# Gated linear attention on one NeuronCore: the scalar engine's side work moved one level behind its exponentials, and every gate made among the first head's levels

## The reference, cut to what matters

```
q, k, v, g, glr, mq = split(hn @ a_w_in)                    # 1024 prompt tokens + 8 sample tokens
log_a = log_sigmoid(glr @ a_w_gate2 + a_b_gate) / 16        # per token, 4 heads x 128 channels
# recurrence, evaluated in chunks:
S_t = diag(exp(log_a_t)) S_{t-1} + k_t^T v_t                # 128 x 192 per head
o_t = q_t S_t
o = rms_norm(o) * silu(g)
```

## Time and profile before

| what | us |
|---|---|
| median of three runs | 2727.14 |
| profiled execution, its own time | 2724.67 |
| span of the profiled execution | 2722.9 |
| PE busy in the span | 2523.3 |
| GLA levels, first scores (404.31) to the last step's transposes (623.83) | 219.5 |
| tail, to the first product of the output projection (650.27) | 26.4 |

### The profile page before, as it was taken

The page is one execution under the profiler, slowest core; times in us unless marked ns, Lnnn a source line. Parts: engine busy times, 40 slices in busy tenths (PEclk is TensorE's granted clock), DMA queues, the critical chain, the costliest instruction groups (busy, mean ns, idle before and its releaser), DMA issues.

```text
span 2722.9 us, 40392 instructions
## 1 busy us (share of the span) xinstructions
PE 2523.3 (93%) x16277; PEld 2413.8 (89%) x16277; DVE 1106.9 (41%) x1685; ACT 510.8 (19%) x1096; POOL 924.1 (34%) x460
## 2 busy tenths in 40 slices
PE   3899977768999999999999789999899999999999
PEld 3899975667999999999999778776899999999998
DVE  6421214645453333333333666623743333333333
ACT  2322113343120000000001434122310000000000
POOL 6333333222323333333334333300233333333332
PEclk9999996889999999999999899979899999999999
DMA  4110131113111111111111310320011111111112
GB/s 174 58 39 32 51 128 36 38 37 130 47 40 47 46 46 46 46 46 46 46 46 47 128 51 32 122 109 1 32 37 47 45 47 45 45 46 46 47 46 75
DMA packets 40994, 154.92 MB, mean 57 GB/s; under 512 B 4784, under 2 KB 11440, under 8 KB 38592
## 3 DMA queue, kind: packets, MB, share of 16 engines
q1 hardware_dynamic: 29760, 107.54, 11.6%
q10 hardware_dynamic: 11136, 45.97, 4.4%
HBM read 135.17 MB, written 18.33 MB: 56 GB/s over the span
## 4 chain that ended last, share of the span: by engine, by line
PE 88%; DVE 8%; ACT 2%; issue 1%; ACTq 0%; DMA 0%; POOL 0%; DVEq 0%; SPq 0%; POOLq 0%
PE bank L576 25%; PE bank L578 25%; PE bank L577 25%; PE bank L770 2%; DVE xt L1664 1%; PE bank L1160 1%; PE bank L1135 1%; PE bank L1155 1%; PE bank L1023 1%; PE bank L1132 1%; PE bank L600 1%; PE bank L655 1%; PE bank L635 1%; PE bank L984 0%; PE bank L643 0%
## 5 line engine op out<-in xcount | busy, mean ns | idle before, releaser
L576 PE MATMUL bank<-x_hi,w_hi 128*128 128x344 f32 (+1 forms) x3304 | 1072.4, 325 | 35.7 <-DVE x_lo L1697 12.5
L577 PE MATMUL bank<-x_lo,w_hi 128*128 128x344 f32 (+1 forms) x3304 | 1058.3, 320 | 0.0
L578 PE MATMUL bank<-x_hi,w_lo 128*128 128x344 f32 (+1 forms) x3304 | 1057.9, 320 | 0.0
L479 POOL TENSOR_TENSOR w_hi<-w_raw,zero 128x1024 fp32r<-128x1024 f32 x187 | 360.9, 1930 | 1534.0 <-PE bank L578 1478.5
L576 PEld LDWEIGHTS bank<-x_hi,w_hi 128*128 128x128 f32 x3304 | 626.6, 190 | 50.8 <-issue 48.0
L577 PEld LDWEIGHTS bank<-x_lo,w_hi 128*128 128x128 f32 x3304 | 625.8, 189 | 1.8 <-issue 0.7
L578 PEld LDWEIGHTS bank<-x_hi,w_lo 128*128 128x128 f32 x3304 | 626.0, 189 | 0.0
L481 POOL TENSOR_TENSOR w_lo<-w_raw,w_hi 128x1024 fp32r<-128x1024 f32 x187 | 461.2, 2466 | 14.7
L1985 DVE TENSOR_TENSOR hid<-sil,bank 128x344 f32<-128x344 f32 x132 | 67.7, 513 | 779.8 <-PE bank L578 742.3
L576 PE MATMUL bank<-hid_hi,w_hi 128*128 128x344 f32 x1056 | 340.1, 322 | 0.0
L577 PE MATMUL bank<-hid_lo,w_hi 128*128 128x344 f32 x1056 | 337.7, 320 | 0.0
(11 more groups left out here) (302 smaller groups left out, 1787.6 us busy)
## 6 DMA issues: line engine op xcount, KB each, us to landing
w_raw<-in_w SPq DMA_DIRECT2D x187, 512.0 KB, 3.4
h<-in_x ACTq DMA_DIRECT2D x3, 1376.0 KB, 15.3
h_spill<-h ACTq DMA_DIRECT2D x1, 4128.0 KB, 11.8
h<-h_spill ACTq DMA_DIRECT2D x1, 4128.0 KB, 13.7
out_y<-h ACTq DMA_DIRECT2D x3, 1376.0 KB, 5.7
g_spill<-ring ACTq DMA_DIRECT2D x6, 516.0 KB, 2.6
h<-in_x ACTq DMA_DIRECT2D x1, 3096.0 KB, 9.9
st_ring<-in_state SPq DMA_DIRECT2D x4, 768.0 KB, 4.3
```

The costliest lines, as they stand in the source:

```text
L479: nc.gpsimd.tensor_tensor(w_hi[:, s], w_raw[:, s], zero[:].broadcast_to([P, 1024]), ALU.add).then_inc(s_whi, 1)
L576: pe.matmul(out, wh, xh, start=(i == 0), stop=False)
L577: pe.matmul(out, wh, xl, start=False, stop=False)
L578: mm = pe.matmul(out, wl, xh, start=False, stop=(i == n - 1))
```

## The change

ACT's loop is split in two functions. `decays(hh, l)` is the exponential of a step, unchanged. `between_decays(hh, l)` is all other ACT work of that step. The loop issues `decays(n)` and then `between_decays(n - 1)`.

The gates of heads 1, 2 and 3 are all made during head 0's nine steps (the last part at step 0 of head 1). For that z of heads 1, 2 and 3 has three buffers (`ring[:, 0]`, `ring[:, 1]` and a new `z_3` that lies in a weight-split slot), and one shared `zt` that lies where `st` is later; `st_ring1` moves by 32 bytes. `cumulate` on DVE is split: the log decays (L1740) are made at steps 4 and 7 of head 0 and 1 of head 1, the scans at step 5 instead of 4. On PE, `sample_values` moves from step 5 to 1, `sample_keys` from 7 to 5, `state_updates` from 1 to 0, `outs` from 3, 4 to 2, 3; `sample_outs` goes from step 0 of the next head but one to step 8. POOL's split of weight tile `U_AOUT` moves behind the levels, since its slot now holds `z_3`.

```diff
-        gate_bufs = [(at("z_0", ...), at("zt_0", ...))] + [(ring[:, 0], ring[:, 1])] * 3
+        zt = at("zt", [P, T], O_X + 57408)
+        gate_bufs = [(at("z_0", ...), at("zt_0", ...))] + [(z, zt[:]) for z in (ring[:, 0], ring[:, 1], at("z_3", [P, T], O_WS + 4096)[:])]
...
@@ POOL
-            split_unit(U_AOUT)
...
+            pool.wait_ge(s_as, H)
+            split_unit(U_AOUT)
             pool.wait_ge(s_clo, A_CLO - 1)
@@ PE gate_products
-                elif hh == 2:
-                    pe.wait_ge(s_sxk, SK_KEYS)
                 else:
-                    pe.wait_ge(s_y, 2 * (hh - 2))
-                    pe.wait_ge(s_sn, 8 * (hh - 2))
+                    pe.wait_ge(s_sxk, SK_VALUES if hh == 2 else SK_KEYS)
@@ PE state_updates, sample_keys
-                pe.wait_ge(s_zb, 3 * min(hh + 3, H))
+                pe.wait_ge(s_zb, 3 * H)
...
             def sample_keys():
+                pe.wait_ge(s_zb, 9)
@@ PE loop
                     level_scores(hh, l)
-                    if l == 0 and hh >= 2:
-                        sample_outs(hh - 2)
-                    if l == 0 and hh + 1 < H:
-                        gate_products(hh + 1)
-                    if hh == 0 and l in (2, 4, 6, 7):
-                        mem_samples(0, (l - 1) // 2 if l < 7 else 3)
-                    if hh == 0 and l == 5:
-                        sample_values()
-                    if hh == 0 and l == 7:
-                        sample_keys()
-                    if hh >= 1:
+                    if hh == 0:
+                        if l in (0, 3, 7):
+                            gate_products({0: 1, 3: 2, 7: 3}[l])
                         if l == 1:
+                            sample_values()
+                        if l == 5:
+                            sample_keys()
+                        if l in (2, 4, 6, 7):
+                            mem_samples(0, (l - 1) // 2 if l < 7 else 3)
+                    else:
+                        if l == 0:
                             state_updates(hh - 1)
-                        if l in (3, 4):
-                            outs(hh - 1, l - 3)
+                        if l in (2, 3):
+                            outs(hh - 1, l - 2)
                         if l in (5, 6):
                             outs_turned(hh - 1, l - 5)
                         if l == 7:
                             sample_updates(hh - 1)
-            sample_outs(H - 2)
+                        if l == 8:
+                            sample_outs(hh - 1)
@@ ACT gates
-                    elif c == 0:
-                        act.wait_ge(s_bc, NBLK * hh)
-                        act.wait_ge(s_as, hh)
...
+                if part == 1 and hh == 1:
+                    act.wait_ge(s_lvl, 1)
+                if part == 1 and hh >= 2:
+                    act.wait_ge(s_la, hh)
@@ ACT loop
+            def between_decays(hh, l):
+                if hh == 0:
+                    if l in (0, 1, 2):
+                        gates(1, l)
+                    if l in (3, 4, 5):
+                        gates(2, l - 3)
+                    if l in (7, 8):
+                        gates(3, l - 7)
+                    if l == 1:
...                                                          # v_one kept (was at 6)
+                    if l in (2, 4):
+                        mem_samples(0, l // 2 - 1)
+                    if l == 5:
...                                                          # k_one kept (was at 8)
+                        sample_decay(1)
+                if hh == 1 and l == 0:
+                    gates(3, 2)
+                if (hh, l) in ((0, 8), (1, 5)):
+                    sample_decay(2 + hh)
+                if l == 4:
...                                                          # b_end, state written (was at 3)
+                if l in (2, 3) and hh >= 1:
+                    outs_normed(hh - 1, l - 2)
+                if l == 8:
+                    keys_kept(hh)
+                    if hh >= 1:
+                        sample_kept(hh - 1)
+            for n in range(NSTEP * H):
+                decays(n // NSTEP, n % NSTEP)
+                if n >= 1:
+                    between_decays((n - 1) // NSTEP, (n - 1) % NSTEP)
@@ DVE
+            def log_decays(hh):
...                                                          # the wait for s_zt and L1740, out of cumulate
+                        if hh == 0:
+                            dve.wait_ge(s_la, H)             # in states, ahead of the first write of st
...
+                    if (hh, l) in ((0, 4), (0, 7), (1, 1)):
+                        log_decays({4: 1, 7: 2, 1: 3}[l])
-                    if l == 2 and hh >= 1:
+                    if l == 1 and hh >= 1:
                         states(hh - 1)
-                    if l == 4 and hh + 1 < H:
+                    if l == 5 and hh + 1 < H:
                         cumulate(hh + 1)
```

More of the change, by code:

```diff
@@ L256, in trunk_program @@
         O_WS = O_W + 12288
-        st_ring = [at("st_ring0", [P, NB, DV], O_X + 28736), at("st_ring1", [P, NB, DV], O_WS + 8192)]
+        st_ring = [at("st_ring0", [P, NB, DV], O_X + 28736), at("st_ring1", [P, NB, DV], O_WS + 8224)]
         k_one = at("k_one", [P, H, 2, P], O_WS)
@@ L260, in trunk_program @@
         v_one = at("v_one", [P, H * DV], O_H + 5 * ROW)
-        gate_bufs = [(at("z_0", [P, T], O_H + 5 * ROW + 5120)[:], at("zt_0", [P, T], O_C + 12608)[:])] + [(ring[:, 0], ring[:, 1])] * 3
+        zt = at("zt", [P, T], O_X + 57408)
+        gate_bufs = [(at("z_0", [P, T], O_H + 5 * ROW + 5120)[:], at("zt_0", [P, T], O_C + 12608)[:])] + [(z, zt[:]) for z in (ring[:, 0], ring[:, 1], at("z_3", [P, T], O_WS + 4096)[:])]
         cks = [at("ck_a", [P, 2, NB, MEM], O_X + 20480), at("ck_b", [P, 2, NB, MEM], O_H)]
@@ L516, in _ @@
                         pool.wait_ge(s_bc, NBLK * (hh + 1))
-                    if hh == 0 and l == 2:
+                    if hh == 0 and l == 1:
                         pool.wait_ge(s_prep, SP_KEYS_CLEAR)
@@ L1406, in sample_kept @@
                 nc.scalar.activation(v_one[:, r * DV:(r + 1) * DV], out, ACT.Copy, scale=o_st[:, 1, r:r + 1]).then_inc(s_sst, 1)
[L1408 to L1448, removed]
@@ new lines, in decays @@
+            def decays(hh, l):
+                n = NSTEP * hh + l
+                if l < NLEV:
+                    act.wait_ge(s_df, NLEV * hh + l + 1)
+                    nc.scalar.activation(dec[:, n % 3], dec[:, n % 3], ACT.Exp, scale=1.0 / TAU).then_inc(s_ex, 1)
+                    return
+                if n >= 3:
+                    act.wait_ge(s_mu, n - 2)
+                b_cum = b_cums[hh % 2]
+                if l == NLEV:
+                    nc.scalar.activation(dec[:, n % 3], b_cum[:], ACT.Exp, scale=1.0 / TAU).then_inc(s_ex, 1)
+                    if hh >= 1:
+                        act.wait_ge(s_ex, NSTEP * hh)
+                    nc.scalar.activation(b_sum[:], b_cum[:, P - 1::P], ACT.Copy, scale=1.0 / TAU).then_inc(s_bs, 1)
+                    return
+                act.wait_ge(s_bs, hh + 1)
+                for b in range(NBLK):
+                    cols = slice(b * P, (b + 1) * P)
+                    op = nc.scalar.activation(dec[:, n % 3, cols], b_cum[:, cols], ACT.Exp, scale=-1.0 / TAU, bias=b_sum[:, b:b + 1])
+                op.then_inc(s_ex, 1)
@@ L1451, in _ @@
                         nc.scalar.activation(v_one[:, 512:768], banks[5][:, 0:256], ACT.Copy).then_inc(s_sxk, 1)
-                    if hh == 0 and l == 8:
+                    if l in (2, 4):
+                        mem_samples(0, l // 2 - 1)
+                    if l == 5:
                         act.wait_ge(s_sx, SX_KEYS)
@@ L1455, in _ @@
                             nc.scalar.activation(k_one[:, 2 * i:2 * i + 2].rearrange("p h m d -> p (h m d)"), banks[4 + i][:], ACT.Copy).then_inc(s_sxk, 1)
-                    if l == 6 and hh + 1 < H:
-                        sample_decay(hh + 1)
+                        sample_decay(1)
[4 more added lines that the diff above has]
+                if l == 4:
+                    if hh >= 1:
+                        act.wait_ge(s_st, NBLK * hh)
+                    nc.scalar.activation(b_end[:], b_cums[hh % 2][:, P - 1::P], ACT.Exp, scale=1.0 / TAU).then_inc(s_be, 1)
+                    if hh >= 1:
+                        act.dma_start(gstate_d[hh - 1], st[:, NBLK - 1]).then_inc(s_gst, 16)
+                if l in (2, 3) and hh >= 1:
+                    outs_normed(hh - 1, l - 2)
+                if l == 8:
+                    keys_kept(hh)
+                    if hh >= 1:
+                        sample_kept(hh - 1)
[3 more added lines that the diff above has]
+                    between_decays((n - 1) // NSTEP, (n - 1) % NSTEP)
             keys_kept(H - 1)
@@ L1734, in mem_attention @@
                     nc.vector.tensor_copy(mq[:, :, i * P:(i + 1) * P], banks[5][:, 0:2 * P].rearrange("p (r m) -> p r m", r=2)).then_inc(s_pok, 1)
-            def cumulate(hh):
```

(6 more changed lines are left out.)

## The result

The changed kernel takes 2704.97 us (median of four runs, 2704.06 to 2706.6) against 2726.61 us of the kernel before beside it: ratio 0.9921, 95% interval 0.9904 to 0.9938. That is 21.6 us less; the forecast was 18 less. A second set gave 2706.6 against 2727.73 us (0.9932, 0.9915 to 0.9948).

What follows compares the result with a forecast made beforehand. The prediction saw a chain of waits between PE, ACT and DVE, with no full engine, from 404 to 650 us. Heads 1 to 3 (14.1 us) plus head 0 (4) made 18 less, 2727.14 to 2709 us; range 2691 to 2720.

Steps and rivals of the forecast that it cites:

- Head starts: Heads 1 to 3: step 2 starts 11.8 us after step 0, for 17.5 in head 1, behind the states on DVE.
- Steps 2 to 5: Heads 1 to 3: 5.8 us from step 2 to 3, 6.4 to 4, 4.4 to 5; moves mostly an exchange.
- Remainder to the next head: From step 5 of head 1 to the next head: 21.7 us for 21.26, with 0.4 of the scan on the path.
- Heads 1 to 3: Heads 1 to 3 together 14.1 us less: 5.4, 5.1 and 3.6.
- Head 0: Head 0, with two more sets of gate products: 4 us less, between bounds of 4.7 more and 11.8 less.
- The clock: PE's granted clock, 0.68 to 0.82 in the four heads before; forecast to stay within 0.74 to 0.88 in heads 1 to 3.
- Tail: The stretch behind the four heads: unchanged, at 26.4 us.
- POOL's moved split, SP's queue, sample outputs: POOL's split, 4.4 us, fits the tail; SP's waits come earlier; sample_outs, 1.25 us, fits PE's 4.24 us wait.
- The clock rival (a): The clock comes back, PE at 2.4 GHz nearly throughout the levels: 41 us less, 2686 us; chance 12%.
- (b): Gates crowd head 0, 4.7 us longer, with 9 to 12 saved elsewhere: 4 to 8 less, about 2721; chance 17%.
- (c): PE at 1.2 GHz sets the pace in heads 1 to 3, steps 2 to 7: 2754 us; chance 5%.
- (d): Some wait of the moved work replaces the gate wait in full: no change within 0.2%, 2725 us; chance 4%.

Runs made afterwards that it cites:

- the old positions: The change with state updates and outputs back at steps 1, 3 and 4, states and norms one step later too: 2698.41 us (0.9897).
- the norm alone is later: The change with the norm of each output half one step later on ACT, behind the exponential of the step after next: 2688.97 us (0.9861).
- the three further edits: The change with norms one step later, states split in halves on DVE and q_one's clearing later on POOL, positions as changed: 2671.69 us (0.9804).
- ACT's order alone: The kernel before, with ACT doing gates and the sample output's norm after the next step's exponential; gates stay in every head: 2706.78 us (0.9926).
- ACT's order undone: The change with ACT making its gate parts ahead of the next exponential again, all else as changed: 2718.94 us (0.9973).
- the halved states: The change with only the states in two halves on DVE: 2691.61 us (0.9871).

## Why the prediction was right

**Head starts** (17.5 us to step 2, forecast 11.8): 11.5, 10.9 and 11.4 us in heads 1 to 3, with the wait for the states ahead of step 2 as forecast. Right.

**Steps 2 to 5** (5.8, 6.4, 4.4): 6.8, 6.4, 4.4 in head 1. Heads 2 and 3 give 5.8 for the first. Right to 0.1 us except in head 1, where the low clock lasted longer: step 2's scores took 3.78 us (3.38 in the earlier trace rows) and the first output products behind them 1.49. The count of waits was right too (1.86 and 2.34 us); what I did not draw from it is that the moved outputs left step 4 bare. Naming the moves an exchange was the wrong reading of right numbers, since I compared them only with the kernel before: with the old positions heads 1 to 3 are 5.8 us shorter still, and the kernel 6.6.

**Remainder to the next head** (21.7): 21.3 in head 1 (482.30 to 503.55). Right.

**Heads 1 to 3**, 14.1 less forecast: 15.7 measured. Head 1 5.2 (5.4), head 2 8.1 (5.1), head 3 2.4 (3.6). The two misses have the clock beside them, 0.84 for 0.79 in head 2 and 0.80 for 0.82 in head 3; I had held it. But head 1's clock rose more, 0.87 for 0.78, and head 1 gave no more than forecast, so the mean clock of a head does not price it.

**Head 0** was the mis-sized term: 4 less, between bounds of +4.7 and -11.8; it is 8.1. The added sets took 2.00 and 3.80 us on PE, 5.8 together for the 7.6 of the upper bound, and the removed wait was sized right, 2.9. What the 4 left out stands in the stretches: idle time fell by 4.9 us in all (16.8 to 11.9), and busy time by 3.2 although 5.8 of gate products came in, so the work that was there before took 9.0 less, at a clock of 0.78 for 0.68. I had put 4 as a value near the middle of two wide bounds, not worked out; that it lies on the right side is in part luck.

**The clock**, held in every other term: 13.4 of the 23.7 us in the heads are shorter busy time for the same work. The forecast of 18 is near 21.6 because the waits on the chain were priced right and the clock moved mainly in head 0, where the 4 us stood for it. The order of events was forecast; the gain from the clock was not.

**Tail**, forecast unchanged: 1.4 us longer to the first product at 627.82. The state updates in it are at the low clock, 4.21 us for 2.87 in the kernel before:

```profile
603.94 4.21 PE L788 MATMUL bank<-v_tok,k_tok 128*128 128x192 f32 x16
```

In the kernel in which the norm alone is later, this stretch is 26.36 us, as before the change.

**POOL's moved split, SP's queue, sample outputs**: no row speaks against their price of nothing. POOL has two instructions and 3.4 us more in head 3 (x9 and 11.86 for x7 and 8.44) and none in the tail: the split ends at 574.07 us, 54 us before its product can start. The sample output ends at 501.96, ahead of step 0 at 503.55.

**Rivals.** The clock rival (a) came only in part with this change, whose heads are at 0.78 to 0.87 for 0.68 to 0.82, and nearly in full in heads 1 and 2 with the three further edits (0.96 and 0.97). "HAM oscillation" in the Trainium skill's page "TensorE: Matmul & The Clock Gate" says that long idle gaps of PE cost it the clock. The runs agree in the direction; the largest gap inside heads 1 and 2 is 2.6 us there, and 3.5 and 2.8 in the change. But head 3 of the last kernel is at 0.85 with no gap above 2.3 us, and head 2 of the kernel with ACT's order alone is at 0.90 with a gap of 4.19 us in it, so the length of the largest gap alone does not decide it. (b), head 0 eats it, and (c), slower, found no support, except that (b)'s place was well chosen: with ACT's order undone head 0 grows by 14.8 us. (d) came in part, as the prediction had it: the wait for the states stands ahead of step 2 in heads 1 to 3, at 3.51, 2.78 and 2.78 us instead of 2.6.

## What to carry to other kernels

In an engine's list, put what feeds the next step ahead of anything that waits for another engine; here ACT's order alone gave 20.0 us, and the same rule for the norms 16 on top of the change. More than half of the first was the clock (14.5 us of PE's busy time) and a third of the second. Judge each edit of a change against the change without it, not only against the kernel before: one part lost 6.6 us inside a gain of 21.6. Where the clock of TensorE is partial, size a removed wait as a wait plus the low-clock time around it, and say both.

## What the runs showed of the hardware that I had not expected

The same list of instructions is granted different clocks from execution to execution. The first gate products of head 0 start 3.7 us after PE does in every kernel; in the profiled execution of the change they took 2.40 us, in that of its repetition 3.81:

```profile
407.87 2.40 PE L683 MATMUL bank<-glr,gate 16*128 16x344 f32 x6
```

```profile
409.28 3.81 PE L683 MATMUL bank<-glr,gate 16*128 16x344 f32 x6
```

In all fourteen profiles these products took one of the two: 2.4 us in the three in which the section starts before 404.6 us, 3.8 in the eleven in which it starts later. Whether the start time is the cause was not tried. And it need not cost anything: head 0 was 49.00 us with the first and 49.30 with the second, since the third set of products then took 2.00 us instead of 3.80.

And head 2, same list, took 47.45 us at 0.90 (gates first) and 50.76 at 0.84 (the change). Differences of up to 3 us in one head of one profile are within what this does. An edit that closed a gap of 2 us per head was worth more than that: the halved states took 6.7 us of idle time away and 3.7 of busy time with it, since step 2's scores took 2.05 us instead of 3.7. I cannot tell from these runs which gap is the one that lets the clock fall. Being busy did not always bring it back: the slice of the earlier trace rows belongs to a longer stretch of head 0, from 434.34 to 446 us, in which PE had no pause and the clock stayed at 0.50; matmuls of 8 rows (`sample_values`) were among its work.
